# Differential attention beside a projection: each head's query tiles taken from the widest to the narrowest

## The chip, the cores and the metric

One core of a Trainium2 chip runs the whole program. The metric is the time of one execution on the device in microseconds (us); the time before is the median of three runs. Engines are written as the profile writes them: PE (TensorE, matrix products), PEld (its weight loads), DVE (VectorE), ACT (ScalarE), POOL (GpSimd), SP (the queue that issues the weight transfers).

## The reference

The program is a small model of three layers on 512 tokens of width 1024 in float32. The first layer begins with a projection `proj = rms_norm(x) @ w_in` (1952 columns), whose first part feeds a causal differential attention of 8 heads. Only this attention is touched:

```
def attn_map(qb, kk):
    sc = jnp.einsum('bhqd,bhkd->bhqk', qb, kk, ...) * scale + bias      # bias = -slope * |distance|
    return jax.nn.softmax(jnp.where(mask, sc, NEG_INF), axis=-1)
a = attn_map(qb1, k1) - lam * attn_map(qb2, k2)
o = jnp.einsum('bhqk,bhkd->bhqd', a.astype(v.dtype), v, ...)
```

Queries come in four tiles of 128. Query tile i sees keys 0 to 128*(i+1), so the score tiles are 128, 256, 384 and 512 columns wide for i = 0 to 3. Each is needed twice, for the two halves (32 features each) of a head. The value product of a head needs all four query tiles. Which of the four is computed first makes no difference to the result.

After it come a latent attention (`mla`), an output projection, a cross attention, a mixture of experts, and a second model part; none of them is edited.

## The kernel before

**Stages.** All engines run one list of stages in order; each stage has its part for PE, ACT and DVE, and each engine takes its own instructions strictly in the order written. Semaphores tie the engines together. A `Linear` stage is a projection in tiles of 128 output columns. A full tile is 24 products of 128x512 on PE (8 slices of the contraction, each as high*high L279, high*low L280, low*high L281). For each tile ACT rounds the weights of the tile after next into `w_high` (L234), DVE subtracts to get `w_low` (L240), and DVE takes the finished product out of PSUM (L675 or L678). On DVE these two stand together: `w_low` first, then the taking-out.

**Places.** The differential attention (`diff`, kind "alibi") is not a stage of its own. It is cut into 35 calls `diff.gap(n)`, n = 0 to 34, here called places. Places 0 to 25 lie in the tiles 2 to 14 of the projection "in": an even place in the middle of a tile (after 12 of its 24 products), an odd place at the end of a tile. Places 26 and 27 lie in the small tile "kpe", 28 to 31 in the projection "uq" and 32 to 34 in "ukv", whose tiles are short (6 or 3 products each). In the middle of a tile, on ACT and DVE, the place comes before the tile's `w_high`, `w_low` and taking-out; at the end of a tile it comes after them.

**What a place does.** A group is one head and one query tile, 32 in all; group n has the two score tiles of its width w. Place n does, on each engine, in this order:

- PE: the two score tiles of group n (L875, four weight loads and products of K = 32, two per score tile); the transposes of group n-2 (L887, one for each 128 columns); if group n-3 was the last of its head, the value products (L903, 8 of them).
- ACT: the copy of the transposes of group n-2 (L955); after every second head the copy of the value product (L962); the two exponentials of group n (L939).
- DVE: reciprocal, scale and combination of the probabilities of group n-1 (L1013, L1018, L1020); then for group n, for each of the two score tiles, bias plus row minimum (L996, written in place into PSUM).

**The one pair of banks.** The scores of all groups go into one pair of PSUM banks (`diff.banks = pairs[1:]`), so the score tile j of group n waits on PE until the exponential j of group n-1 has read the bank (L873, `need(pe, "att_act", ("exp", before, ...))`). PE is in order, so everything behind it waits too. Every eighth place also has four transposes of values (L713, copied at L722), and single operations of other work are hung on fixed places: angles for the later rotary embedding (L1206 to L1224, on DVE at places 4, 6, 8, 10, 12, 14), squares for norms (L388, on ACT at places 4, 12, 20), the roots of two norms with table loads on ACT (L441, L1229, place 22).

The order of the groups is the list `self.groups` in `Attention.__init__` (L742 to L746). Everything else (which place, which bank, which buffer) goes by the group's number. The last entry of a group, the list `closes`, says after which group the head's value products may run.

Of the kernel before, what the change touches and what calls it, by code (L numbers as in the profile page):

```python
# [28 lines left out]
QT = S // P  # L29
# [85 lines left out]
class Events:  # L115
# [12 lines left out]
    def done(self, ins, name, label=None, by=1):  # L128
        ins.then_inc(self.sem(name), by)
        self.count[name] = self.count.get(name, 0) + by  # L130
        if label is not None:
            self.seen[name, label] = self.count[name]
# [7 lines left out]
    def need(self, eng, name, label):  # L140
        self.wait(eng, name, self.plan[name, label])
# [7 lines left out]
def program(nc, a, plan):  # L149

    with ExitStack() as ctx:
# [94 lines left out]
        class Linear:  # L246
# [3 lines left out]
            def __init__(self, name, high, low, ready, take_act=None, take_dve=None, before=None, beside=None,  # L250
                         opening=None, middle=None):
                self.opening, self.middle = opening, middle or {}
                self.name, self.high, self.low, self.ready = name, high, low, ready
                self.beside = beside or {}
                self.take_act, self.take_dve, self.before = take_act, take_dve, before
                _, self.nt, self.kt, self.m, self.n = STAGE_OF[name]
                self.base = BASE[name]
# [471 lines left out]
        class Attention:  # L729
# [5 lines left out]
            def __init__(self, name, heads, kind, scale, scores, probs, turned, pv, out, wait_scores, wait_v,  # L735
                         next_tile, wait_out=None, per_tile=2, outs=None, after=None, lazy=False):
                self.outs, self.after, self.beside, self.wait_values = outs or (ps_o, ps_m), after, {}, {}
                self.name, self.heads, self.kind, self.scale = name, heads, kind, scale
                self.scores, self.probs, self.turned, self.per_tile = scores, probs, turned, per_tile
                self.pv, self.out, self.wait_scores, self.wait_v = pv, out, wait_scores, wait_v  # L740
                self.wait_out, self.next_tile = wait_out, next_tile
                wide_ = [(h, i) for h in range(heads) for i in range(QT)]  # L742
                if kind == "alibi":
                    self.groups = [([(h, i, 0), (h, i, 1)], (i + 1) * P,
                                    [(h, i, [(0, b) for b in range(i + 1)])], [h] if i == QT - 1 else [])
                                   for h, i in wide_]  # L746
                elif kind == "causal":
                    self.groups = [([(h, i, 0), (h + 1, i, 0)], (i + 1) * P,
                                    [(h + r, i, [(r, b) for b in range(i + 1)]) for r in range(2)],
                                    [h, h + 1] if i == 0 else [])  # L750
                                   for h in range(0, heads, 2) for i in reversed(range(QT))]
                else:
                    self.groups = [([(h, i, 0) for i in range(QT)], 2 * P,
                                    [(h, b, [(i, b) for i in range(QT)]) for b in range(2)], [h])
                                   for h in range(heads)]
                self.m0, self.h0, self.o0 = seen_groups["n"], seen_heads["n"], seen_outs["n"]
                self.u0, self.opened = [0] * len(self.groups), []
                if not lazy:
                    for n in range(len(self.groups)):
                        self.number(n)  # L760
                sizes.extend(len(group[0]) for group in self.groups)
                seen_groups["n"] += len(self.groups)
                seen_heads["n"] += heads
                seen_outs["n"] += heads // per_tile
                self.last = ("att_act", ("out", seen_outs["n"] - 1))
                self.banks = pairs
# [178 lines left out]
            def act_turn(self, act, n):  # L945
                for q, (h, i, blocks) in enumerate(self.groups[n][2]):
                    u = self.u0[n] + q
                    need(act, "turn_pe", u)
                    if n == 0 and q == 0 and self.wait_out:
                        self.wait_out(act)  # L950
                    if i == (QT - 1 if self.kind == "causal" else 0) and h >= len(self.turned):

                        need(act, "att_pe", ("values", self.h0 + h - len(self.turned)))
                    dst, src = self.place_turned(h, i, len(blocks))
                    done(act.copy(dst, src(ps_t[u % 2])), "turn_act", u)  # L955
# [2394 lines left out]
```

How the kernel before makes its waits and increments, by code:

```python
    def wait(self, eng, name, value):  # L134
        if self.waited.get((id(eng), name), 0) < value:
            eng.wait_ge(self.sem(name), value)
            self.waited[id(eng), name] = value
# [78 lines left out]
        def wait_evac(eng, t):  # L217
            eng.wait_ge(evacuated[t % BANKS], t // BANKS + 1)
# [7 lines left out]
        def wait_products(eng, name):  # L226
            eng.wait_ge(tile_done, BASE[name] + STAGE_OF[name][1])
# [1 line left out]
        def split_high(act, t):  # L229
            _, _, kt, m, _ = TILE[t]
            act.wait_ge(w_loaded[t % RING], 16 * (t // RING + 1))
            if t >= SPLIT:
                act.wait_ge(tile_done, t - SPLIT + 1)
            act.activation(WH[:, t % SPLIT, 0:kt * m], WRAW[:, t % RING, 0:kt * m],
                           ACT.Copy).then_inc(high_ready, 1)
# [1 line left out]
        def split_low(dve, t):  # L237
            _, _, kt, m, _ = TILE[t]
            dve.wait_ge(high_ready, t + 1)
            dve.tensor_tensor(WL[:, t % SPLIT, 0:kt * m], WRAW[:, t % RING, 0:kt * m],
                              WH[:, t % SPLIT, 0:kt * m].bitcast(F32), ALU.subtract).then_inc(low_ready, 1)
# [23 lines left out]
            def tensor_tile(self, pe, j):  # L265
                while scores_read:
                    need(pe, *scores_read.pop())
                t = self.base + j
                pe.wait_ge(low_ready, t + 1)
                if t >= BANKS:
                    wait_evac(pe, t - BANKS)
                out = ps_lin[t % BANKS][0:self.m, 0:self.n]
# [1687 lines left out]
        def store_y(act, b):  # L1960
            act.wait_ge(y_taken, b + 1)
            for n in range(2):
```

## Time and profile before

| what | value |
|---|---|
| device time, median of 3 runs | 2140.44 us (2137.41 to 2144.48) |
| span of the profiled execution | 2139.1 us |
| PE busy | 1953.0 us (91%) |
| DVE busy | 1079.6 us (50%) |
| ACT busy | 792.7 us (37%) |
| mean granted TensorE clock | 0.955 |

The span is the time from the first to the last instruction of one profiled execution. No device time is listed for that one execution; its span lies 1.3 us under the median of the three runs. Places 0 to 31 fall between 34.9 us and 195 us of the span, which is 7% of it. "Busy" of PE counts a product until its modelled end, so short waits between products can hide in it. PE's clock has two levels, 1.2 and 2.4 GHz, shown as a granted clock of 0.50 and 1.00.

### The profile page before, as it was taken

To read this page: it belongs to the slowest core of one execution; us is meant where nothing else is said; L and a number is where in the kernel's file an instruction comes from. 1 tells how busy PE (TensorE), PEld (TensorE's weight loads), DVE (VectorE), ACT (ScalarE), POOL (GpSimd) and SP (SyncE) were. 2 spreads that over 40 slices of the span, in tenths; PEclk is the share of its full clock that TensorE was granted. 3 is DMA by queue.
4 is the path that set the end of the run, shared out by engine and by line. 5 is a ranking of instruction groups with operands and counts; after the bars stand their busy time and mean duration, and the time that the engine had idled before them with its cause. 6 is when DMAs were issued, how large, how long until landed. Compare 5 with 4: busy or idle time off the path is not lost.

```text
span 2139.1 us, 25847 instructions
## 1 busy us (share of the span) xinstructions
PE 1953.0 (91%) x10050; PEld 1526.5 (71%) x10050; DVE 1079.6 (50%) x2000; ACT 792.7 (37%) x1653; POOL 118.9 (6%) x85
## 2 busy tenths in 40 slices
PE   7999998859877769999989999999998999999997
PEld 5665667646544457788987888788876778888886
DVE  6767655452211137685564444644556554434344
ACT  4456644532211136633543321322423643222222
POOL 0000000000000034020420000000000000000000
PEclk9999999979999969999999999999998899999999
DMA  5102313439999951112002222232220022222321
GB/s 187 35 12 79 111 55 116 149 125 387 411 412 406 405 196 60 62 67 69 1 1 68 95 99 89 90 108 90 98 93 17 1 74 94 99 98 82 107 89 48
DMA packets 78394, 261.10 MB, mean 122 GB/s; under 512 B 9377, under 2 KB 11681, under 8 KB 77889
## 3 DMA queue, kind: packets, MB, share of 16 engines
q1 hardware_dynamic: 68112, 231.47, 30.2%
q0 software_dynamic: 5040, 19.58, 2.8%
q10 hardware_dynamic: 5120, 8.39, 1.1%
q8 instruction: 81, 1.33, 0.2%
q14 instruction: 41, 0.33, 0.0%
HBM read 242.62 MB, written 16.79 MB: 121 GB/s over the span
## 4 chain that ended last, share of the span: by engine, by line
PE 71%; DMA 8%; DVE 7%; ACT 3%; issue 2%; POOL 0%; SPq 0%; ACTq 0%; DVEq 0%; POOLq 0%
PE ps_pair L279 17%; PE ps_pair L281 17%; PE ps_pair L280 17%; DMA split_acts_as_f<-w_experts 7%; PE ps_pair L875 3%; PE ps_pair L1983 3%; PE ps_turn L2491 2%; PE ps_out L903 2%; PE ps_turn L887 2%; PE ps_pair L2491 1%; PE ps_shared L903 1%; DMA w_raw<-w_mem 1%; PE ps_pair L2496 1%; PE ps_shared L1994 1%; PE ps_turn L2496 1%
## 5 line engine op out<-in xcount | busy, mean ns | idle before, releaser
L279 PE MATMUL ps_pair<-split_acts,w_high 128*128 128x512 f32 (+1 forms) x1816 | 718.0, 395 | 25.3 <-DVE split_acts L608 9.9
L281 PE MATMUL ps_pair<-split_acts,w_low 128*128 128x512 f32 (+1 forms) x1816 | 705.8, 389 | 0.0
L280 PE MATMUL ps_pair<-split_acts,w_high 128*128 128x512 f32 (+1 forms) x1800 | 699.3, 389 | 0.0
L240 DVE TENSOR_TENSOR w_low<-w_raw,w_high 128x1024 fp32r<-128x1024 f32 (+5 forms) x257 | 291.9, 1136 | 295.3 <-ACT w_high L234 293.3
L279 PEld LDWEIGHTS ps_pair<-split_acts,w_high 128*128 128x128 f32 x1816 | 344.3, 190 | 104.2 <-issue 22.3
L281 PEld LDWEIGHTS ps_pair<-split_acts,w_low 128*128 128x128 f32 x1816 | 343.9, 189 | 71.9
L280 PEld LDWEIGHTS ps_pair<-split_acts,w_high 128*128 128x128 f32 x1800 | 342.0, 190 | 66.2 <-issue 0.2
L234 ACT ACTIVATE w_high<-w_raw 128x1024 fp32r<-128x1024 f32 (+5 forms) x257 | 251.2, 978 | 193.6 <-PE ps_pair L281 168.6
L1983 PE MATMUL ps_pair<-split_acts_as_f 128*64 128x256 f32 x512 | 126.5, 404 | 40.5 <-DMA split_acts_as_f<-w_experts 39.1
L1985 PE MATMUL ps_pair<-split_acts_as_f 128*64 128x256 f32 x512 | 127.0, 405 | 0.0
L354 DVE TENSOR_TENSOR x<-x,ps_pair 128x512 f32<-128x512 f32 x80 | 55.0, 687 | 139.5 <-PE ps_pair L281 139.5
L1983 PEld LDWEIGHTS ps_pair<-split_acts_as_f 128*64 128x64 f32 x512 | 71.9, 146 | 74.3 <-issue 47.8
L939 ACT ACTIVATE g<-ps_pair,columns 128x256 f32<-128x256 f32 (+3 forms) x176 | 86.8, 506 | 40.3 <-DVE columns L996 34.5
L2157 DVE TENSOR_TENSOR g<-g,ps_pair 64x256 f32<-64x256 f32 x31 | 13.2, 425 | 172.9 <-ACT g L2097 172.8
L3039 ACT ACTIVATE split_acts<-h 128x512 fp32r<-128x512 f32 x44 | 27.9, 633 | 192.4 <-DVE h L3052 192.4
L875 PE MATMUL ps_pair<-g 64*128 64x256 f32 (+5 forms) x288 | 77.5, 471 | 13.5 <-ACT g L939 7.9
L3034 ACT ACTIVATE h<-h 128x512 f32<-128x512 f32 x44 | 27.8, 632 | 134.8 <-DVE h L3045 134.8
L955 ACT COPY split_acts_as_f<-ps_turn 128x512 f32<-128x512 f32 (+3 forms) x104 | 49.7, 507 | 70.2 <-PE ps_turn L887 65.8
L875 PEld LDWEIGHTS ps_pair<-g 32*128 32x128 f32 (+2 forms) x288 | 46.0, 207 | 37.5 <-ACT g L939 14.9
L1985 PEld LDWEIGHTS ps_pair<-split_acts_as_f 128*64 128x64 f32 x512 | 71.9, 146 | 0.0
L3049 DVE TENSOR_TENSOR h<-ps_pair,h 128x512 f32<-128x512 f32 x44 | 30.4, 691 | 73.7 <-PE ps_pair L281 73.7
L887 PEld LDWEIGHTS ps_turn<-consts,g 128*128 128x128 f32 x320 | 38.0, 149 | 34.9 <-issue 14.6
(482 smaller groups left out, 2283.4 us busy)
## 6 DMA issues: line engine op xcount, KB each, us to landing
split_acts_as_f<-w_experts SPq DMA_DIRECT2D x192, 512.0 KB, 14.0
w_raw<-w_gu SPq DMA_DIRECT2D x88, 512.0 KB, 3.4
w_raw<-w_down SPq DMA_DIRECT2D x32, 448.0 KB, 3.2
w_raw<-w_gdnin SPq DMA_DIRECT2D x26, 512.0 KB, 3.5
w_raw<-w_out SPq DMA_DIRECT2D x24, 512.0 KB, 3.5
rows_y<-scratch ACTq DMA_DIRECT2D x64, 128.0 KB, 6.3
w_raw<-w_down SPq DMA_DIRECT2D x16, 512.0 KB, 3.4
w_raw<-w_in SPq DMA_DIRECT2D x15, 512.0 KB, 3.8
```

The costliest lines, as they stand in the source:

```text
L234: act.activation(WH[:, t % SPLIT, 0:kt * m], WRAW[:, t % RING, 0:kt * m], ACT.Copy).then_inc(high_ready, 1)
L240: dve.tensor_tensor(WL[:, t % SPLIT, 0:kt * m], WRAW[:, t % RING, 0:kt * m], WH[:, t % SPLIT, 0:kt * m].bitcast(F32), ALU.subtract).then_i ...
L279: pe.matmul(out, wh[:, k, :], self.high(k), start=(k == 0), stop=False)
L280: pe.matmul(out, wh[:, k, :], self.low(k), start=False, stop=False)
L281: last = pe.matmul(out, wl[:, k, :], self.high(k), start=False, stop=(k == self.kt - 1))
L875: done(pe.matmul(self.member(self.bank(m), j, w), lhs, rhs, start=True, stop=True, skip_group_check=True), "att_pe", ("scores", m, j))
L887: last = pe.transpose(ps_t[u % 2][:, at_ * P:(at_ + 1) * P], src, ident)
L903: last = pe.matmul(self.outs[o % len(self.outs)][rows, q0:q1], lhs, self.turned[h % len(self.turned)][:, slot, src:src + q1 - q0], start=f ...
L939: done(act.activation(self.member(self.prob(n), j, w), self.member(self.bank(m), j, w), ACT.Exp, bias=COL[:, c + j:c + j + 1], scale=self. ...
L1983: pe.matmul(out[rows, 0:256], xs, w[:, at_:at_ + 256], start=(k == 0), stop=(k == KT - 1), skip_group_check=True)
L1985: last = pe.matmul(out[high_rows, 0:256], xs, w[:, at_ + 256:at_ + 512], start=(k == 0), stop=(k == KT - 1), skip_group_check=True)
L2491: last = pe.matmul(pair(bank)[:, n, :], lhs(h), rhs(h), start=True, stop=True)
```

## The change

The groups of a head now run from query tile 3 (512 columns) down to query tile 0 (128 columns). The head closes with tile 0, and the guard that keeps a head from overwriting the transposed probabilities of two heads before moves to the head's first group, now tile 3. Nothing else is edited; the sum of work is the same on every engine.

```diff
@@ -742,8 +742,8 @@
                 wide_ = [(h, i) for h in range(heads) for i in range(QT)]
                 if kind == "alibi":
                     self.groups = [([(h, i, 0), (h, i, 1)], (i + 1) * P,
-                                    [(h, i, [(0, b) for b in range(i + 1)])], [h] if i == QT - 1 else [])
-                                   for h, i in wide_]
+                                    [(h, i, [(0, b) for b in range(i + 1)])], [h] if i == 0 else [])
+                                   for h in range(heads) for i in reversed(range(QT))]
                 elif kind == "causal":
@@ -948,7 +948,7 @@
                     if n == 0 and q == 0 and self.wait_out:
                         self.wait_out(act)
-                    if i == (QT - 1 if self.kind == "causal" else 0) and h >= len(self.turned):
+                    if i == (0 if self.kind == "full" else QT - 1) and h >= len(self.turned):
 
                         need(act, "att_pe", ("values", self.h0 + h - len(self.turned)))
                     dst, src = self.place_turned(h, i, len(blocks))
```

What stands on ACT from place 4 to place 6, before. L955 is the copy of the transposes, L939 the two exponentials, L388 a square for a norm, L234 the rounding of the next weights.

```order
L955 COPY split_acts_as_f_51<-ps_turn 128x3x128
L939 ACTIVATE g,columns<-ps_pair,columns 128x128 x2
L388 ACTIVATE h<-g 128x512
L234 ACTIVATE w_high<-w_raw 128x1024
L955 COPY split_acts_as_f_51<-ps_turn 128x4x128
L939 ACTIVATE g,columns<-ps_pair,columns 128x256 x2
L955 COPY split_acts_as_f_51<-ps_turn 128x128
L939 ACTIVATE g,columns<-ps_pair,columns 128x384 x2
```

The same stretch of ACT after the change:

```order
L955 COPY split_acts_as_f_51<-ps_turn 128x2x128
L939 ACTIVATE g,columns<-ps_pair,columns 128x512 x2
L388 ACTIVATE h<-g 128x512
L234 ACTIVATE w_high<-w_raw 128x1024
L955 COPY split_acts_as_f_51<-ps_turn 128x128
L939 ACTIVATE g,columns<-ps_pair,columns 128x384 x2
L955 COPY split_acts_as_f_51<-ps_turn 128x4x128
L939 ACTIVATE g,columns<-ps_pair,columns 128x256 x2
```

The exponentials ahead of `w_high` (L234) are now 512 wide instead of 128, those behind it 384 instead of 256.

What stands on DVE at the end of the same tile (place 5), before: `w_low`, the taking-out of the product, the probabilities of group 4, the biased scores of group 5.

```order
L240 TENSOR_TENSOR w_low<-w_raw,w_high 128x1024
L675 SCALAR_TENSOR_TENSOR g<-ps_pair,columns,h 128x512
L1013 RECIPROCAL columns<-columns 128x1
L1018 SCALAR_TENSOR_TENSOR columns<-columns 128x1
L1020 SCALAR_TENSOR_TENSOR g<-g,columns 128x128
L996 ISA ps_pair,columns<-split_acts_as_f_51,ps_pair 128x256
L996 ISA columns 128x1
L996 ISA ps_pair,columns<-split_acts_as_f_51,ps_pair 128x256
L996 ISA columns 128x1
```

The same stretch of DVE after the change:

```order
L240 TENSOR_TENSOR w_low<-w_raw,w_high 128x1024
L675 SCALAR_TENSOR_TENSOR g<-ps_pair,columns,h 128x512
L1013 RECIPROCAL columns<-columns 128x1
L1018 SCALAR_TENSOR_TENSOR columns<-columns 128x1
L1020 SCALAR_TENSOR_TENSOR g<-g,columns 128x512
L996 ISA ps_pair,columns<-split_acts_as_f_51,ps_pair 128x384
L996 ISA columns 128x1
L996 ISA ps_pair,columns<-split_acts_as_f_51,ps_pair 128x384
L996 ISA columns 128x1
```

The combination of the probabilities is 512 wide instead of 128, the two biased score tiles are 384 wide instead of 256. The same holds at places 1, 9, 13, 17, 21 and 25. At places 3, 7, 11 and so on it is the other way round: 256 and 128 wide instead of 384 and 512.

## Rows read from the trace of the kernel before

**Rows 1.** The page's shares of the chain that ended last, by engine.

```profile
PE 71%; DMA 8%; DVE 7%; ACT 3%; issue 2%; POOL 0%; SPq 0%; ACTq 0%; DVEq 0%; POOLq 0%
```

**Rows 2.** Groups by form, PE, 34.9 to 200 us: busy us, mean ns, idle before.

```profile
L875 PE MATMUL ps_pair<-g 32*128 32x384 f32 x32 | 9.5, 533 | 1.3 <-ACT g L939 1.3
L875 PE MATMUL ps_pair<-g 32*128 32x512 f32 x32 | 9.0, 640 | 0.0
L875 PE MATMUL ps_pair<-g 32*128 32x128 f32 x32 | 6.3, 320 | 2.8 <-ACT g L939 2.4
L875 PE MATMUL ps_pair<-g 32*128 32x256 f32 x32 | 5.9, 426 | 0.2 <-ACT g L939 0.2
```

**Rows 3.** Timeline of PE, places 18 and 19: start us, us, operation.

```profile
118.68 0.92 PE L875 MATMUL ps_pair<-g 32*128 32x384 f32 x4
119.53 0.33 PE L887 MATMUL ps_turn<-consts,g 128*128 128x128 f32 x1
119.79 2.37 PE L903 MATMUL ps_out<-split_acts_as_f,g 128*64 128x512 f32 x8
...
125.42 1.13 PE L875 MATMUL ps_pair<-g 32*128 32x512 f32 x4
126.47 0.44 PE L887 MATMUL ps_turn<-consts,g 128*128 128x128 f32 x2
...
129.28 0.39 PE L281 MATMUL ps_pair<-split_acts,w_low 128*128 128x512 f32 x1
```

**Rows 4.** Timeline of all engines, from `w_high` of place 18 to place 20.

```profile
124.26 1.09 ACT L234 ACTIVATE w_high<-w_raw 128x1024 fp32r<-128x1024 f32 x1
...
125.38 1.23 DVE L240 TENSOR_TENSOR w_low<-w_raw,w_high 128x1024 fp32r<-128x1024 f32 x1 [4.62 <-ACT w_high L234]
126.52 0.69 DVE L678 TENSOR_TENSOR g<-ps_pair,h 128x512 f32<-128x512 f32 x1
...
127.57 0.62 DVE L1020 SCALAR_TENSOR_TENSOR g<-g,columns 128x384 f32<-128x384 f32 x1
128.10 0.69 DVE L996 CUSTOM_DVE_ANT_0 ps_pair<-split_acts_as_f,ps_pair 128x512 f32<-128x512 f32 x1
...
128.71 0.73 DVE L996 CUSTOM_DVE_ANT_0 ps_pair<-split_acts_as_f,ps_pair 128x512 f32<-128x512 f32 x1
...
128.95 0.69 ACT L939 ACTIVATE g<-ps_pair,columns 128x512 f32<-128x512 f32 x1 [1.62 <-DVE columns L996]
...
130.45 0.48 PE L875 MATMUL ps_pair<-g 32*128 32x128 f32 x2 [0.19 <-ACT g L939]
```

**Rows 5.** Timeline: the other widths on DVE and ACT.

```profile
119.63 0.56 DVE L996 CUSTOM_DVE_ANT_0 ps_pair<-split_acts_as_f,ps_pair 128x384 f32<-128x384 f32 x1 [0.21 <-PE ps_pair L875]
...
123.24 0.58 ACT L939 ACTIVATE g<-ps_pair,columns 128x384 f32<-128x384 f32 x1
...
130.88 0.75 DVE L1020 SCALAR_TENSOR_TENSOR g<-g,columns 128x512 f32<-128x512 f32 x1
```

**Rows 6.** Timeline: other work hung on places 8 and 20.

```profile
73.38 0.42 DVE L1222 TENSOR_SCALAR scratch<-g 128x512 f32<-128x512 f32 x1
...
76.21 1.22 DVE L240 TENSOR_TENSOR w_low<-w_raw,w_high 128x1024 fp32r<-128x1024 f32 x1
...
132.69 0.62 ACT L388 ACTIVATE h<-g 128x512 f32<-128x512 f32 x1
```

**Rows 7.** Timeline of ACT: the first exponential of place 0.

```profile
38.06 0.37 ACT L939 ACTIVATE g<-ps_pair,columns 128x128 f32<-128x128 f32 x1 [8.09 <-DVE columns L996]
```

**Rows 8.** Timeline of PE: place 24.

```profile
152.03 1.06 PE L875 MATMUL ps_pair<-g 32*128 32x128 f32 x4 [1.18 <-ACT g L939]
```

**Rows 9.** Timeline of PE: the first scores of the latent attention.

```profile
215.65 1.22 PE L875 MATMUL ps_pair<-g,split_acts_as_f 96*128 96x512 f32 x1 [1.29 <-ACT split_acts_as_f L1449]
```

**Rows 10.** Windows: length, busy us of PE, PEld, DVE, ACT, POOL (instructions), granted clock, DMA share, GB/s.

```profile
19.70:26.50 6.80, 6.80 (x25) 5.93 (x25) 2.90 (x8) 1.21 (x3) 0.00 (x0) 0.50 0.83 301
150.60:152.10 1.50, 0.32 (x3) 0.10 (x1) 0.03 (x1) 1.49 (x4) 0.00 (x0) 1.00 0.00 0
```

## The prediction

> **What bounds the kernel now.** I read the page's chain of work first. PE holds 71% of it and every other engine 8% or less [rows 1], so a change in the attention's order is worth what it changes in PE's waits. PE does the same products after the change. I therefore looked only at places 0 to 31 and asked where PE waits there.
>
> The groups by form answer it [rows 2]. PE waits before the scores for the exponential (L939) that frees the banks. The idle time in front of L875 is 1.3 us at the 384-wide groups, 2.8 at the 128-wide, 0.2 at the 256-wide and 0.0 at the 512-wide, 4.3 us together. More hides in the busy column. The two score tiles of a group run side by side when both may start: the 384-wide group takes 119.53 - 118.68 = 0.85 us in all [rows 3]. If the second is let go late, it alone takes the full time again. Eight undisturbed 384-wide groups would be 8 x 0.92 = 7.4 us, and the row has 9.5 us. Eight undisturbed 128-wide groups would be about 3.9 us (0.49 each, shorter than the 512-wide 1.13 of [rows 3] by 3 x 0.21) and the row has 6.3. With 0.3 for the 256-wide groups that is 4.8 us more, so PE loses about 9.1 us to this wait. Followed place by place with the walk below I get 9.9 us. It falls into three parts:
> - the 128-wide groups that open a head (places 4, 12, 20, 24, 28): 5.5 us,
> - the 384-wide groups in third position (places 2, 6, 10, 14, 22): 3.8 us,
> - the start (place 1): 0.6 us.
>
> **The change, part by part.** The sum of work of each engine stays. What moves is which width stands before an odd place (behind `w_low` and the taking-out) and which before an even one. I walk the loop that PE waits for, with steps from start to start.
>
> *Lengths.* Scores of 512 take 1.05 and of 384 0.85 [rows 3]. By the same slope (0.21 for each 128 columns) it is 0.63 for 256 and 0.42 for 128. DVE starts on scores 0.10 after they end: 119.63 - 118.68 = 0.95 [rows 3, 5]. One transpose takes 0.26, two take 0.19 [rows 3]; three or four I take as 0.31 and 0.42. From the start of two transposes to the last projection product is 129.28 - 126.47 = 2.81, and 0.32 more to the next scores [rows 3], so twelve products take 2.94. `w_low` starts 1.12 after `w_high` and takes 1.14, the taking-out 0.60, reciprocal and scale 0.45. The 384-wide combination takes 0.53, the first 512-wide biased tile 0.61, and 0.24 after it ends ACT starts the exponential, 0.68 for each 512-wide one [rows 4]. The 512-wide combination takes 0.67, the 384-wide tiles about 0.50 each and the 384-wide exponentials 0.57 [rows 5]. PE starts 0.15 after an exponential ends: 128.95 + 2 x 0.68 + 0.15 = 130.46, and the second scores start at 130.45 [rows 4].
>
> *The wait that goes.* In the old order place 3 (mod 4) has 384-wide probabilities and 512-wide scores and exponentials behind the taking-out. In [rows 4] this loop ends at 130.45, and PE was ready at 129.60 [rows 3]: a wait of 0.85. After the change these widths are 256 and 128 there, so the loop is shorter by 0.13 for the probabilities, 0.39 for the first tile (the second lies beside the first exponential) and 0.66 for the two exponentials. `w_high` in front of it stands behind 256-wide exponentials instead of 384-wide ones and comes another 0.22 earlier. That is 1.40, while PE's own path is shorter by 0.64 - 0.12 = 0.52. The room grows by 0.88, the wait was 0.85. So places 4, 12, 20 and 28 lose their wait. Place 24 keeps some: the table load in front of its exponential stays, and 1.8 us (1.18 idle, and 1.06 busy where 0.49 would do [rows 8]) becomes about 1.0. With 0.36 of small rests in places 4, 12 and 20, the first part goes from 5.5 to 1.3 us, a gain of 4.2.
>
> *The wait that comes.* Now take a head in the new order, with its 512-wide scores starting at T in the middle of a tile. The biased tiles run from T+1.15 to T+2.41, the exponentials from T+2.0 to T+3.36. Only then comes `w_high`, so `w_low` starts at T+4.48 and ends at T+5.62, the taking-out ends at T+6.22. PE has reached the end of the tile at T + 1.05 + 0.19 + 2.94 = T+4.18, two microseconds before. Behind the taking-out now stand 0.45 + 0.67 for 512-wide probabilities, to T+7.33; the first 384-wide tile, and its exponential starts at T+8.05; the second ends at T+9.20, and PE may start its second scores at T+9.35. PE is there at T + 4.18 + 0.85 + 0.26 + 2.92 = T+8.21. It waits 1.14 us. In the old order the same walk with 128, 256 and 384 gives the second scores free at T+6.9 and PE there at T+7.6, so no wait, which is what place 18 shows: 0.92 for the group, no idle time [rows 3].
>
> Other work adds to it. L388 on ACT (0.53, places 4, 12, 20) delays `w_high` and lifts places 6, 14 and 22 to about 1.5, 1.65 and 1.65. The angle steps at place 8 hold DVE for 76.21 - 73.38 = 2.83 us [rows 6], to T+5.24 instead of T+4.48, and lift place 10 to 1.9. Place 18 has the bare 1.15, place 26, with narrow weight tiles, 0.95. At the start DVE is late anyway: the first exponential starts at 38.06 [rows 7] and would now start at 38.45, being 512 wide; place 1 waits 1.1 and place 2 about 2.1. So third positions go from 3.8 to 10.9 us, a loss of 7.1, and place 1 loses 0.5.
>
> *The end.* In "uq" the tiles are short and the places far apart, so the same loop has over 0.5 us of room at each; I add nothing. In "ukv" ACT is the engine that PE waits for, up to 1.29 us before the first scores of the next attention [rows 9]. There the last group is now 128 wide, which takes 2 x 0.33 us of exponentials and 0.3 of copies off ACT, but DVE arrives there later by up to 0.9. I take -0.4, bounds 0 and -1.0.
>
> *Sum.* -4.2 + 7.1 + 0.5 - 0.4 = **+3.0 us**. Against the profiled span that is 2142.1. The median of the runs shown lies 1.3 us higher, so 2143.4, which I round to 2143.5. That is +0.14%. What a measurement of this kernel can tell from no change is about 0.3%, or 6.4 us.
>
> **The rivals.**
>
> *PE's clock falls in the new waits, and the kernel is measurably slower.* After the 3.9 us that PE waits for norm squares near 16 us, the granted clock is at its lower level, 1.2 GHz, from 19.7 to 26.5 us [rows 10]. One such stretch costs half of 6.8, 3.4 us. Against it: at place 24 PE idled 1.18 us and stayed at 1.00 [rows 8, 10]. For it: places 2, 10 and 22 now lose 1.6 to 2.1 us each. One fall makes +6.4, 2146.9, just at the bound; two make 2150. It decides from the first fall on, since +3.0 alone stays inside. The Trainium skill, "TensorE: Matmul & The Clock Gate", section "What's actually happening", has the clock gate go by how busy PE has been recently; by it the sum is 3.4 us more for each fall, by the row of place 24 nothing. Chance 0.2.
>
> *The opening waits go and nothing takes their place, a gain.* It holds if `w_low` is not late at the odd places. With it 1 us earlier the wait of 1.14 is gone, and the kernel gains 4.2 + 0.4: 2135.8. For it speaks that in the old order place 18 passes without a wait [rows 3]. Against it: ACT can't start `w_high` before a 512-wide exponential has ended, which is fixed by the order. Even so it is less than the bound; only with the spread of the runs would it show. Chance 0.12.
>
> *The waits only change places.* PE's delay at one place gives DVE and ACT time to catch up before the next, and the total stays near 9.9: 2140.4, give or take 1.5. For it: the sums of widths over a tile pair are the same in both orders. Chance 0.13.
>
> **How the numbers follow.** My forecast, wait moved and 3.0 us longer, has 0.55. Its own range is 2141 to 2146: the error of the walk is at most 0.8 over all places where I can set it beside the old trace, and the end is open by 0.6. The range for 8 in 10 goes from the middle of the gain (2138) to between one and two clock falls (2149). Slower by over 0.3%: nearly all of the clock rival plus a few hundredths of the forecast's upper tail, 0.22. Faster by over 0.3%: only the gain rival's lower tail with the spread of 7 us that three runs show, 0.06. Within 0.3%: 0.72.
>
> **What would show it right or wrong.** In the profile after, L875 at 128 columns should show almost no idle time and about 4 us busy except place 24. L875 at 256 columns should carry the idle time, ahead of it exponentials of 384 columns, with busy time well over 5.9 us, and some 13 us lost in all. L240 should start after PE has ended its tile at places 5, 9, 13, 17 and 21. The first scores of the latent attention should start near 218.6 us instead of 215.65 [rows 9]. I am wrong if the 256-wide groups start without a wait, if the clock row has a stretch at 0.50 between 40 and 200 us, or if the attention ends where it did and the time moves elsewhere.

## The result, and the profile after

The changed kernel is slower, by a little more than one measurement can tell from nothing.

| what | before | after |
|---|---|---|
| device time, median | 2140.18 us (2137.09 to 2145.57, 10 runs) | 2150.22 us (2145.91 to 2151.28, 10 runs) |
| ratio of runs taken side by side | 1 | 1.0039, 95% interval 1.003 to 1.0049 |
| span of the profiled execution | 2139.1 us | 2146.2 us |
| mean granted TensorE clock | 0.955 | 0.951 |

The ratio is +8.3 us (0.0039 x 2140), with an interval from +6.4 to +10.5. The forecast was +3.0. A slowdown of more than 0.3% was given a chance of 0.22 in all.

The groups by form of PE over the same stretch as [rows 2]: busy us, mean ns of one, idle before.

```profile
L875 PE MATMUL ps_pair<-g 32*128 32x512 f32 x32 | 9.6, 639 | 0.9 <-ACT g L939 0.9
L875 PE MATMUL ps_pair<-g 32*128 32x256 f32 x32 | 9.1, 426 | 7.1 <-ACT g L939 7.1
L875 PE MATMUL ps_pair<-g 32*128 32x384 f32 x32 | 8.0, 533 | 0.3 <-ACT g L939 0.3
L875 PE MATMUL ps_pair<-g 32*128 32x128 f32 x32 | 3.9, 321 | 0.0
```

The wait has moved as the prediction said. It left the 128-wide groups (2.8 idle and 6.3 busy before, 0.0 and 3.9 now) and the 384-wide ones, and stands at the 256-wide groups, which had 0.2 and 5.9 and now have 7.1 and 9.1.

One of these waits in full, on the timeline of all engines from the scores of place 5 to the transposes of place 6:

```profile
59.38 1.05 ACT L234 ACTIVATE w_high<-w_raw 128x1024 fp32r<-128x1024 f32 x1
59.68 0.91 PE L875 MATMUL ps_pair<-g 32*128 32x384 f32 x4
...
60.53 1.22 DVE L240 TENSOR_TENSOR w_low<-w_raw,w_high 128x1024 fp32r<-128x1024 f32 x1 [1.26 <-ACT w_high L234]
61.67 0.74 DVE L675 SCALAR_TENSOR_TENSOR g<-ps_pair,columns,h 128x512 f32<-128x512 f32 x1
...
62.77 0.75 DVE L1020 SCALAR_TENSOR_TENSOR g<-g,columns 128x512 f32<-128x512 f32 x1
63.44 0.55 DVE L996 CUSTOM_DVE_ANT_0 ps_pair<-split_acts_as_f,ps_pair 128x384 f32<-128x384 f32 x1
...
64.15 0.58 ACT L939 ACTIVATE g<-ps_pair,columns 128x384 f32<-128x384 f32 x1 [2.99 <-DVE columns L996]
64.72 0.57 ACT L939 ACTIVATE g<-ps_pair,columns 128x384 f32<-128x384 f32 x1
64.87 1.26 PE L875 MATMUL ps_pair<-g 32*128 32x256 f32 x4 [1.26 <-ACT g L939]
66.06 0.44 PE L887 MATMUL ps_turn<-consts,g 128*128 128x128 f32 x2
```

Read it upwards. The 256-wide scores wait for the 384-wide exponentials; these wait for DVE's bias tile (L996); and that stands behind the 512-wide probabilities, the taking-out and `w_low`, which starts 0.85 us after the scores of place 5 because `w_high` came late.

PE's loss at a place is taken from the trace in one way for every kernel below: the start of the first operation behind the group's scores (a transpose from place 2 on), less the start of the last product ahead of them, less 0.32 (that product), less the time that the scores take when nothing holds them (0.42, 0.63, 0.85 or 1.06 by width, rounded here). At place 6 the last product starts at 63.23, so it is 66.06 - 63.23 - 0.32 - 0.63 = 1.88. Over places 0 to 31 the changed kernel loses 13.6 us and the old one 9.9, so the waits cost +3.7.

The clock gives nearly all of the rest of what is lost ahead of the latent attention. In windows with the columns of [rows 10]:

```profile
43.80:47.20 3.40, 2.14 (x13) 1.31 (x12) 2.54 (x11) 1.26 (x5) 0.00 (x0) 1.00 0.34 133
47.20:50.60 3.40, 3.40 (x12) 2.72 (x11) 0.94 (x5) 2.92 (x7) 0.00 (x0) 0.50 0.00 0
34.90:210.00 175.10, 165.65 (x731) 104.69 (x730) 120.81 (x333) 84.03 (x224) 0.00 (x0) 0.99 0.11 32
```

The wait of place 2 lies in the first window, where PE is busy for 2.14 of 3.40 us. Behind it the granted clock is 0.50 for 3.4 us, the lower of the two levels (1.2 GHz). Such a stretch did not exist between 30 and 200 us before:

```profile
34.90:210.00 175.10, 169.55 (x759) 107.81 (x758) 122.56 (x338) 89.06 (x234) 0.00 (x0) 1.00 0.14 42
```

Half of 3.4 is 1.7 us. The first scores of the latent attention, which closed [rows 9] at 215.65, now start here:

```profile
221.31 1.22 PE L875 MATMUL ps_pair<-g,split_acts_as_f 96*128 96x512 f32 x1 [1.29 <-ACT split_acts_as_f L1449]
```

That is 5.66 later: 3.7 of waits, 1.7 of clock and 0.2 from ahead of the attention, whose first scores start at 35.07 us instead of 34.90:

```profile
35.07 1.13 PE L875 MATMUL ps_pair<-g 32*128 32x512 f32 x4
```

From the first scores of place 0 to those of the latent attention it is 186.24 us instead of 180.75, so 5.49 longer. This distance is the better measure, since the start of place 0 moves from profile to profile. The spans differ by 7.1.

### The profile page after: what moved, and what is told of

Same layout as the page of the kernel before. It is cut to its first block, busy times and chain, and to the rows that moved or that the text cites. A ratio compares the mean times of both kernels' runs of the same rounds, so it can differ in the third digit from the quotient of the medians.

```text
span 2146.2 us, 25837 instructions
## 1 busy us (share of the span) xinstructions
PE 1960.8 (91%) x10050; PEld 1530.9 (71%) x10050; DVE 1081.1 (50%) x2000; ACT 792.7 (37%) x1653; POOL 117.0 (5%) x85
## 4 chain that ended last, share of the span: by engine, by line
PE 76%; DVE 9%; DMA 8%; ACT 4%; issue 2%; POOL 0%; ACTq 0%; DVEq 0%; SPq 0%; POOLq 0%
PE ps_pair L279 18%; PE ps_pair L281 18%; PE ps_pair L280 18%; DMA split_acts_as_f<-w_experts 6%; PE ps_pair L875 4%; PE ps_pair L1983 3%; PE ps_out L903 3%; PE ps_turn L2491 2%; PE ps_turn L887 2%; PE ps_pair L2491 1%; PE ps_shared L903 1%; ACT g L939 1%; DVE ps_pair L996 1%; ACT w_high L234 1%; DVE w_low L240 1%
## 5 line engine op out<-in xcount | busy, mean ns | idle before, releaser
L234 ACT ACTIVATE w_high<-w_raw 128x1024 fp32r<-128x1024 f32 (+5 forms) x257 | 251.3, 978 | 192.1 <-PE ps_pair L281 168.6
L1983 PE MATMUL ps_pair<-split_acts_as_f 128*64 128x256 f32 x512 | 132.3, 418 | 40.7 <-DMA split_acts_as_f<-w_experts 38.1
L1985 PE MATMUL ps_pair<-split_acts_as_f 128*64 128x256 f32 x512 | 132.8, 418 | 0.0
L1983 PEld LDWEIGHTS ps_pair<-split_acts_as_f 128*64 128x64 f32 x512 | 74.5, 151 | 77.8 <-issue 46.5
L939 ACT ACTIVATE g<-ps_pair,columns 128x256 f32<-128x256 f32 (+3 forms) x176 | 86.8, 506 | 47.9 <-DVE columns L996 41.8
L875 PE MATMUL ps_pair<-g 64*128 64x256 f32 (+5 forms) x288 | 77.5, 471 | 17.4 <-ACT g L939 12.2
L955 ACT COPY split_acts_as_f<-ps_turn 128x512 f32<-128x512 f32 (+3 forms) x104 | 49.7, 507 | 69.7 <-PE ps_turn L887 65.1
L875 PEld LDWEIGHTS ps_pair<-g 32*128 32x128 f32 (+2 forms) x288 | 45.6, 207 | 41.7 <-ACT g L939 19.6
L1985 PEld LDWEIGHTS ps_pair<-split_acts_as_f 128*64 128x64 f32 x512 | 74.4, 151 | 0.0
L2097 ACT ACTIVATE g<-ps_pair 64x256 f32<-64x256 f32 x31 | 11.7, 376 | 141.0 <-PE ps_pair L1985 141.0
```

Of the source, the lines that this page charges most:

```text
L234: act.activation(WH[:, t % SPLIT, 0:kt * m], WRAW[:, t % RING, 0:kt * m], ACT.Copy).then_inc(high_ready, 1)
L875: done(pe.matmul(self.member(self.bank(m), j, w), lhs, rhs, start=True, stop=True, skip_group_check=True), "att_pe", ("scores", m, j))
L939: done(act.activation(self.member(self.prob(n), j, w), self.member(self.bank(m), j, w), ACT.Exp, bias=COL[:, c + j:c + j + 1], scale=self. ...
L1983: pe.matmul(out[rows, 0:256], xs, w[:, at_:at_ + 256], start=(k == 0), stop=(k == KT - 1), skip_group_check=True)
L1985: last = pe.matmul(out[high_rows, 0:256], xs, w[:, at_ + 256:at_ + 512], start=(k == 0), stop=(k == KT - 1), skip_group_check=True)
```

## The experiments

All ratios are to the old kernel run beside the experiment, and "later" and "earlier" speak of the first scores of the latent attention against the 215.65 of [rows 9]. Place 0 starts anywhere from 33.84 to 36.10 us in the ten profiles, so "the attention takes" gives the distance from the first scores of place 0 to the first scores of the latent attention: 180.75 us in the old kernel, 186.24 in the changed one.

### Head 0 in the old order

Only the seven other heads are turned, to see how much of the loss is the start, where DVE is late anyway. Against the changed kernel, without the line of the guard, which follows `ORDER` too:

```diff
+        ORDER = lambda h: (0, 1, 2, 3) if h == 0 else (3, 2, 1, 0)
...
-                                    [(h, i, [(0, b) for b in range(i + 1)])], [h] if i == 0 else [])
-                                   for h in range(heads) for i in reversed(range(QT))]
+                                    [(h, i, [(0, b) for b in range(i + 1)])], [h] if i == ORDER(h)[-1] else [])
+                                   for h in range(heads) for i in ORDER(h)]
```

> The changed kernel, but head 0 keeps the old order (128 to 512 columns); heads 1 to 7 run from 512 to 128. The waits at places 1 and 2 should be the old ones (0.6 and 1.4 us instead of 1.1 and 1.9), the stretch of lower granted clock at 47 us of the span should be gone, the waits at places 6, 10, 14, 18 and 22 should stay at 1.3 to 2.0 us each. Theory (waits moved to the third place of a head, plus one clock fall in head 0): 1.0 us of waits and 1.7 us of clock are given back, about 2147.5 by the median of the changed kernel. Rival (the loss comes from the order in all heads alike, the clock fall costs nothing): 2149.5. Rival (the loss is made later in the expert stage, whatever the attention does): no different from 2150.

Measured: 2147.2 us (2143.76 to 2151.37, 12 runs), ratio 1.0031 (1.002 to 1.0041), +6.6 us. The waits come to 13.1 us and the latent attention starts at 219.48. Places 1 and 2 went back to the old kernel's 0.6 and 1.4, but place 4, where an old-order head meets a 512-wide group, waits 0.8, so the waits fall by only 0.6. The clock does not fall near 47 us now; it falls once later, at 143.5 us. So most of the loss is not the start's, and where the clock falls is not tied to place 2. The median is close to the 2147.5 of the theory, but not for its reason: 0.6 us of waits came back where it had 1.0, and the fall moved where it was to go. The interval overlaps that of the changed kernel. Place 0 starts early here:

```profile
33.84 0.49 PE L876 MATMUL ps_pair<-g 32*128 32x128 f32 x4
```

The attention takes 219.48 - 33.84 = 185.64 us, 4.9 more than in the old kernel, and that is its 3.2 of added waits and 1.7 for one fall.

### `w_low` behind the attention's work, in both orders

On DVE the tiles 2 and up of the projection "in" now do the taking-out, then the place's own DVE work, and only then `w_low`. It takes `w_low` out of the loop that PE waits for. The same edit is made to the changed kernel and to the old one, in `Linear.vector`:

```diff
+                    if self.name == "in" and j > 1:
+                        self.take_dve(dve, j, self.base + j, ps_lin[(self.base + j) % BANKS][0:self.m, 0:self.n])
+                        for stage in self.beside.get(j, ()):
+                            stage.vector(dve)
+                        split_low(dve, self.base + j + AHEAD)
+                        continue
```

> The changed kernel, but in the tiles 2 to 14 of the projection in, DVE makes w_low of the tile after next only behind the place at the end of the tile, not in front of it. If w_low, late because of the 512-wide exponentials ahead of w_high, is what PE waits for in the third place of a head, the waits of 1.3 to 2.0 us there fall to 0 to 0.8 us, the 13.6 us of waits over places 0 to 31 to about 3 us, and the time by about 10 us from the changed kernel, to 2140. If only the 512-wide probabilities and 384-wide score tiles behind it count (1.11 us more DVE and ACT work in the loop than in the old order), the waits fall by less than half: 2146. If the loss sits elsewhere, no change: 2150.

> The old order, with the same move of w_low behind the place at the end of a tile. The waits should fall from 9.9 to about 2 us (place 1 at 0.7, place 24 at 1.2) and the time by about 8 us, to 2132. With e2 beside it: if w_low in the loop is what makes the two orders differ, the distance between the orders shrinks to about 1 us of waits, plus what the clock makes of them; if the order costs for another reason, it stays at 5 us or more in the first 300 us of the span.

Measured, changed order: 2134.32 us (2132.12 to 2141.02, 12 runs), ratio 0.9973 (0.9961 to 0.9984), clearly under the 2140 expected. Old order: 2134.15 us (2129.61 to 2138.44, 7 runs), ratio 0.9962 (0.9948 to 0.9976). The waits fall to 3.8 and 2.8 us, and neither has a stretch at 0.50 between 30 and 200 us. PE by form, changed order with `w_low` last (the edit moves L875 to L881, L939 to L945 and L996 to L1002):

```profile
L881 PE MATMUL ps_pair<-g 32*128 32x512 f32 x32 | 9.6, 639 | 0.2 <-ACT g L945 0.2
L881 PE MATMUL ps_pair<-g 32*128 32x384 f32 x32 | 8.0, 533 | 0.3 <-ACT g L945 0.3
L881 PE MATMUL ps_pair<-g 32*128 32x256 f32 x32 | 6.9, 427 | 0.4 <-ACT g L945 0.3
```

The 256-wide groups' 7.1 us of idle time is 0.4, and their busy time is 6.9 instead of 9.1. The timeline of place 5 shows how:

```profile
57.74 0.55 DVE L1002 CUSTOM_DVE_ANT_0 ps_pair<-split_acts_as_f,ps_pair 128x384 f32<-128x384 f32 x1
...
58.45 0.58 ACT L945 ACTIVATE g<-ps_pair,columns 128x384 f32<-128x384 f32 x1 [1.19 <-DVE columns L1002]
...
58.73 1.22 DVE L240 TENSOR_TENSOR w_low<-w_raw,w_high 128x1024 fp32r<-128x1024 f32 x1
...
59.64 0.79 PE L881 MATMUL ps_pair<-g 32*128 32x256 f32 x4
```

The bias tiles now stand ahead of `w_low`, the first exponential starts before it, and the next scores start with no wait. The places 0 and the first scores of the latent attention:

```profile
34.66 1.13 PE L881 MATMUL ps_pair<-g 32*128 32x512 f32 x4
209.73 2.93 PE L881 MATMUL ps_pair<-g,split_acts_as_f 96*128 96x512 f32 x3 [1.10 <-ACT split_acts_as_f L1455]
```

```profile
36.10 0.49 PE L881 MATMUL ps_pair<-g 32*128 32x128 f32 x4
209.67 2.93 PE L881 MATMUL ps_pair<-g,split_acts_as_f 96*128 96x512 f32 x3 [1.29 <-ACT split_acts_as_f L1455]
```

The first pair is the changed order, the second the old one. That both reach the latent attention at nearly the same moment (0.06 us apart) is chance: the old order began its places 1.44 us later in this profile. The attention takes 175.07 us in the changed order and 173.57 in the old one. So the place of `w_low` makes most of the difference between the orders: with it in the loop they are 5.5 us apart (one clock fall of 1.7 included), with it out of the loop 1.5, of which 1.0 are the waits that are left (3.8 against 2.8). Both kernels beat the one before, by some 6 and 8 us. The two kernels in the changed order are 14 us apart by their ratios (1.0039 and 0.9973); 9.8 of that are waits, and the rest fits two to three clock falls, which was not shown apart.

### The old kernel with a plain delay

The clock and the places behind the attention can change if it merely ends later. So 24 products are added to the old kernel in the output projection behind it, and nothing else.

```diff
+                    for _ in range(24 if self.name == "out" and j == 3 and k == 0 else 0):
+                        pe.matmul(out, wh[:, k, :], self.high(k), start=True, stop=True)
```

> The kernel before, with 24 more products of 128x512 on PE in tile 3 of the output projection (they write the same first partial product again, so that the result is the same), 24 x 0.228 = 5.5 us of work that keeps PE busy and moves everything behind it. If what stands behind the attention passes a shift on unchanged, the span and the median grow by 5.5 us, to 2145.7. If the stages behind (the experts, whose clock and transfers differ between executions) react to when they start, it grows by clearly more or less than 5.5, up to 10 us.

Measured: 2145.92 us (2144.11 to 2151.9, 12 runs), ratio 1.0027 (1.0017 to 1.0036), +5.8 us for 24 products, 0.23 us from start to start, which is 5.5 us. The waits of the attention stay at 9.9 us and its end at 215.65. So a delay here passes to the end about one to one, within the interval of +3.6 to +7.7 us, and what the change costs in the attention must be most of its cost.

### The waits filled with products

If the clock falls because PE waits, filling the six longest waits with products that nobody uses should bring back the clock and leave the waits' own cost. The added products read weights and activations that are there anyway and write into the bank that the place's transposes overwrite.

```diff
+                fill = {2: 6, 6: 5, 10: 6, 14: 5, 18: 3, 22: 5}.get(n, 0) if self.kind == "alibi" else 0
+                if fill:
+                    u = self.u0[n - 2]
+                    if u >= 2:
+                        need(pe, "turn_act", u - 2)
+                    tile = BASE["in"] + 2 + n // 2
+                    for _ in range(fill):
+                        pe.matmul(ps_t[u % 2][:, :], WH[:, tile % SPLIT, 0:P], hi(0), start=True, stop=True)
```

> The changed kernel, but PE fills most of the wait in front of the scores at places 2, 6, 10, 14, 18 and 22 with 3 to 6 extra products of 128x512 (0.228 us each, 30 in all) into a bank of transposes that is written anew right behind; they change no result. The waits as seen from place to place stay, only PE is busy in them. The profile of the changed kernel has one stretch of lower clock at 47 us, behind the wait at place 2. Theory (waits of 1.8 us and more let the clock fall now and then, so the attention costs more than its waits): no fall between 30 and 200 us, the attention ends 1.7 us earlier than in the changed kernel's profile (219.6 instead of 221.3), and the median is 2 to 5 us under that of the changed kernel: 2145 to 2148. Rival (the clock costs nothing beyond the one profile): 2150. Rival (the fill delays the scores): later than 2150.

Measured: 2144.27 us (2141.67 to 2148.39, 12 runs), ratio 1.0019 (1.0009 to 1.0029), +4.1 us. Place 6 on the timeline of PE, the filler at L878 and the scores at L883:

```profile
62.53 1.29 PE L878 MATMUL ps_turn<-split_acts,w_high 128*128 128x512 f32 x5
63.83 1.25 PE L883 MATMUL ps_pair<-g 32*128 32x256 f32 x4
65.02 0.66 PE L895 MATMUL ps_turn<-consts,g 128*128 128x128 f32 x4
```

Over the whole stretch, with the columns of [rows 10], and at its end:

```profile
34.90:210.00 175.10, 172.49 (x770) 110.40 (x768) 121.60 (x337) 85.02 (x227) 0.00 (x0) 1.00 0.12 36
```

```profile
220.45 2.07 PE L883 MATMUL ps_pair<-g,split_acts_as_f 96*128 96x512 f32 x2 [1.10 <-ACT split_acts_as_f L1457]
```

No stretch between 30 and 200 us is below 1.00. With 30 products more to do the kernel is 4.2 us shorter than without them (1.0019 against 1.0039), and the two intervals do not meet; that of the second measurement of the changed kernel, below, overlaps the filled one's by 0.0004. It starts the latent attention 4.8 us later than the old kernel, but its place 0 started late as well:

```profile
35.64 1.13 PE L883 MATMUL ps_pair<-g 32*128 32x512 f32 x4
```

The attention takes 184.81 us, 4.1 more than in the old kernel, of which 3.7 are the waits. Against the first profile of the changed kernel it takes 1.4 us less, with the same waits (13.6 us) and one fall less.

The Trainium skill, "TensorE: Matmul & The Clock Gate", section "What's actually happening", says that the gate follows how busy PE has lately been. The traces agree in part: 2.14 of 3.40 us busy is followed by 0.50, and with the waits filled there is no fall; but a like busy share does not always bring one: the old kernel's place 24, shown further down, has 2.10 of 3.40 and stayed at 1.00.

### `w_high` ahead of the middle place

The other half of the loop is that `w_high` stands behind the 512-wide exponentials. Here ACT does it first, in tiles 2 to 11, in `Linear.scalar`:

```diff
                 for j in range(self.nt):
+                    early = self.name == "in" and 1 < j < 12
+                    if early:
+                        split_high(act, self.base + j + AHEAD)
                     for stage in self.middle.get(j, ()):
                         stage.scalar(act)
-                    self.scalar_tile(act, j)
+                    if not early:
+                        self.scalar_tile(act, j)
```

> The changed kernel, but in the tiles 2 to 11 of the projection in, ACT makes w_high at the start of a tile, in front of the exponentials of the place in its middle. w_low stays where it is, in the loop at the end of the tile, but is no longer late. If its lateness is the cause, the waits at places 2, 6, 18 and 22 fall from 1.9, 1.9, 1.3 and 1.8 us to 0.5 or less; those at 10 and 14 stay at 1.7 to 2.0, since there the angle steps hold DVE anyway. Sum of the waits 8 instead of 13.6, time 2144 to 2145. If the 512-wide probabilities and the presence of w_low in the loop do it, whether late or not: waits stay above 11 us, 2149.

Measured: 2144.15 us (2140.02 to 2151.76, 12 runs), ratio 1.0017 (1.0005 to 1.0028), +3.6 us. PE's 256-wide groups:

```profile
L879 PE MATMUL ps_pair<-g 32*128 32x256 f32 x32 | 8.1, 429 | 3.9 <-ACT g L943 3.9
```

Places 2 and 18 lose nothing now and place 6 loses 0.7, but places 10 and 14 keep 2.1 and 1.9, and place 22 keeps its 1.8. The last is no surprise once seen: `w_low` ahead of place 22 belongs to tile 12, which the edit leaves alone, and I had expected it to go. At place 10 the angle steps ahead of `w_low` [rows 6] hold DVE whatever ACT does. The result is useful in another way. The waits come to 9.3 us, less than the old kernel's 9.9, and the latent attention still starts 2.84 us later, at 218.49. The clock falls twice, at 81.3 and 142.8 us, for 3.4 us each: -0.6 + 2 x 1.7 = 2.8. So the total of the waits does not decide. With three of them at 1.8 to 2.1 us, 9.3 us of waits cost more here than 9.9 us with one that long.

### Both kernels again

The same two kernels once more, since one profile can't say how often the clock falls.

> The changed kernel once more, for a second profile and more times. Waits of places 0 to 31 again 13.6 us, the same to 0.3 us, since they follow from the order. The stretches of lower clock between 30 and 200 us may lie elsewhere and be none to three; each moves the end of the attention by 1.7 us. If the one fall of the first profile is typical, the attention ends near 221.3 again; if the fall was an accident, near 219.6; if falls are more frequent than that profile shows, 223 or later. What the expert stage (560 to 900 us) adds may differ by 3 us either way.

> The kernel before once more, for a second profile: waits of 9.9 us in places 0 to 31, no or one stretch of lower clock in them (place 2 or 24), the first scores of the latent attention at 215.7 us. If the first profile had a lucky expert stage, the stretches of lower clock between 560 and 900 us add up to more than its 55 us, and the span is up to 3 us over 2139.

Measured, changed kernel: 2149.06 us (2142.78 to 2155.14, 12 runs), ratio 1.0038 (1.0025 to 1.005), span 2151.9. Old kernel: one run at 2137.99, span 2136.2. Windows of the changed kernel, with the columns of [rows 10]:

```profile
46.20:49.60 3.40, 3.40 (x13) 2.99 (x13) 1.27 (x5) 2.12 (x7) 0.00 (x0) 0.51 0.00 0
66.60:70.00 3.40, 3.40 (x6) 1.16 (x6) 3.29 (x8) 2.40 (x6) 0.00 (x0) 0.50 0.00 0
148.60:152.00 3.40, 3.40 (x7) 1.11 (x6) 0.73 (x4) 2.79 (x6) 0.00 (x0) 0.51 0.00 0
```

```profile
224.46 1.22 PE L875 MATMUL ps_pair<-g,split_acts_as_f 96*128 96x512 f32 x1 [1.29 <-ACT split_acts_as_f L1449]
```

The waits are the same (13.6 us), but the clock falls three times instead of once: 3.7 + 3 x 1.7 = 8.8, and 224.46 - 215.65 = 8.81. The old kernel again waits 9.9 us and has no fall in this stretch. Its latent attention starts at 216.35, 0.7 later, because its place 0 started 0.76 later. Behind the attention its two profiles also differ, by 3.0 us at 357 us, where the first has been at the low clock for 6.8 us more since 260 us, and by up to 4.9 us in the expert stage. From the first scores of the latent attention to the end, the profiles take between 1919.8 and 1927.5 us. A comparison of single spans can be off by several us, then, and the ratios have to carry the verdict.

With these runs the falls can be counted against the waits. The two profiles of the changed kernel, the one with head 0 in the old order and the one with `w_high` first have 16 waits of 1.8 us or more between them, at places 2, 6, 10, 14 and 22. All seven falls that these four profiles have between 30 and 200 us stand at the end of one of the 16 or just behind it: twice behind place 2, once each behind 6 and 10, three times behind 22, never behind 14. No fall stands behind a shorter wait of these four profiles. The old kernel has one wait of that size, 1.8 us at place 24, and stayed at the full clock behind it in all three of its profiles (the plain delay's among them). The first of them, in a window at that place:

```profile
150.00:153.40 3.40, 2.10 (x11) 1.34 (x10) 1.27 (x7) 2.54 (x5) 0.00 (x0) 1.00 0.00 0
```

PE is no busier there than ahead of the fall at 47.2 us. A wait of this size is a chance of a fall, then, not a fall.

All ten profiles together, in us. "Takes" is the distance from place 0 to the latent attention, "explained" the waits over 9.9 plus 1.7 for each fall:

| kernel | place 0 | latent attention | takes | against 180.75 | waits | falls | explained |
|---|---|---|---|---|---|---|---|
| old | 34.90 | 215.65 | 180.75 | 0 | 9.9 | 0 | 0 |
| old, again | 35.66 | 216.35 | 180.69 | -0.1 | 9.9 | 0 | 0 |
| old, plain delay behind | 34.97 | 215.65 | 180.68 | -0.1 | 9.9 | 0 | 0 |
| old, `w_low` last | 36.10 | 209.67 | 173.57 | -7.2 | 2.8 | 0 | -7.1 |
| changed | 35.07 | 221.31 | 186.24 | +5.5 | 13.6 | 1 | +5.4 |
| changed, again | 34.89 | 224.46 | 189.57 | +8.8 | 13.6 | 3 | +8.8 |
| changed, head 0 old | 33.84 | 219.48 | 185.64 | +4.9 | 13.1 | 1 | +4.9 |
| changed, `w_low` last | 34.66 | 209.73 | 175.07 | -5.7 | 3.8 | 0 | -6.1 |
| changed, filled | 35.64 | 220.45 | 184.81 | +4.1 | 13.6 | 0 | +3.7 |
| changed, `w_high` first | 34.97 | 218.49 | 183.52 | +2.8 | 9.3 | 2 | +2.8 |

The two that are off by 0.4 (`w_low` last in the changed order, and filled) have a fall of 6.8 us that begins further ahead of the latent attention than in the others, and 0.25 us more between the last transposes and its first scores.

## Why the prediction was right on the waits and wrong on the clock

**The loop and its lengths: right.** The walk gave 13.3 us of waits in the changed kernel and the trace has 13.6. By parts: places 2, 6, 10, 14, 18, 22 and 26 were put at 10.9 and lose 11.0; place 1 was put at 1.1 and loses 1.06; the openings were put at 1.3 and lose 1.6 (place 24 1.2, place 28 0.4). The closeness of the total is in part luck, since single places missed in both directions: place 26 was put at 0.95 and loses 0.16, while place 6 was put at 1.5 and loses 1.89, places 14 and 22 at 1.65 and lose 1.89 and 1.80, and place 28 was to lose nothing. The old kernel's 9.9 was right as well. The experiment with `w_low` last confirms the mechanism: once it has left the loop, 9.8 of the 13.6 us go, and 7.1 of the old order's 9.9.

**The end: wrong by 0.4.** I took -0.4 for "ukv". Waits, clock and the later start of place 0 explain the whole 5.66 us, with no gain at the end. This is inside the bounds given (0 to -1.0).

**The clock: the step that failed.** The sum had no term for the clock, and a stretch at 0.50 between 40 and 200 us was named as a sign that I am wrong; it came. The prediction set against a fall that "at place 24 PE idled 1.18 us and stayed at 1.00", and gave the rival 0.2. That one place stayed up was read as a rule, where it was one draw: place 24 loses 1.8 us in all, much like the new waits of 1.8 to 2.0, and behind 16 waits of that size in the reordered kernels the clock fell seven times. The old order has one of them, the new one five (places 2, 6, 10, 14 and 22), so at 7 in 16 each an execution has 2.2 falls, and one without any is rare (9/16 to the fifth, 0.06). This is an estimate: it takes the five waits as alike and independent, while place 22 had three falls behind four such waits and place 14 none behind four. The chance of the rival should have been well over a half. The price was wrong the other way: the one stretch that was read was 6.8 us long and was priced at 3.4, these are 3.4 long and cost 1.7. The filled kernel, which has none, says the same from the times: it is 4.2 us shorter, which is two to three falls, and the intervals leave room for one to four.

The old trace also held a sign for the rival that I passed over. Ahead of the latent attention PE waits three times within 5 us, the third time as shown in [rows 9], and the clock falls there:

```profile
211.24 0.66 PE L713 MATMUL ps_turn<-consts,split_acts_as_f 128*128 128x128 f32 x4 [0.84 <-ACT split_acts_as_f L349]
213.70 0.66 PE L713 MATMUL ps_turn<-consts,split_acts_as_f 128*128 128x128 f32 x4 [1.81 <-ACT split_acts_as_f L349]
```

```profile
210.90:214.30 3.40, 1.25 (x8) 0.84 (x8) 2.16 (x2) 3.33 (x7) 1.40 (x2) 1.00 0.60 165
214.30:221.10 6.80, 5.51 (x8) 2.52 (x8) 1.99 (x6) 2.81 (x7) 0.00 (x0) 0.50 1.00 358
```

No single wait there is longer than 1.81 us. It would not have settled the chance, since PE is less busy there than at the new waits (1.25 us of 3.40), but it stands against place 24.

**The total.** +3.7 of waits and 2.2 x 1.7 of clock give 7.4; measured 8.3 (6.4 to 10.5). My forecast of +3.0 with its own range of 2141 to 2146 is below that. The range for 8 in 10, up to 2149, holds the ratio (2140.4 + 8.3 = 2148.7) only by the room that it left for clock falls, and not the median of 2150.22. The clock rival, which stood on the right side of the bound, is what happened, with two smaller falls where it counted one or two large ones.

**The other rivals.** A gain needed `w_low` not to be late; it was (60.53 against PE's 59.68), and with `w_low` out of the way the gain appeared (0.9973). That the waits only change places is refuted by 13.6 against 9.9, the same in two profiles.

**Open.** How often the clock falls in an execution that isn't profiled was not counted, only inferred from the ratios and from a rate of 7 in 16 that rests on four profiles. What makes one wait lower the clock and the next not was not tried either. What moves the start of place 0 by up to 2.3 us between profiles, and the rest of the program behind the latent attention by up to 7.7, lies outside the stretch read here. What is left between the orders once `w_low` is out of the loop was not taken apart either.

## What to carry to other kernels

When one engine is the bound and waits on a loop through others, look for work in that loop that the loop does not need: here `w_low`, needed a tile later, cost 7.1 us of waits in one order and 9.8 in the other, more than the 3.7 between the orders, and moving it brought them from 5.5 to 1.5 us apart. Price a new wait twice, once for its own length and once for what the clock may do behind it, and look at the longest waits and not at their total alone, since a smaller total with three long pieces was slower; that the clock stayed up behind one wait in one profile is little evidence that it will behind five. Before two profiles are compared at one moment, take off the difference in their start: without that, two kernels that are 1.5 us apart looked equal. A walk from start to start with lengths from the old trace was good to 0.3 us in all over thirty places, and to 0.8 at the worst single one.

## What the runs showed of the hardware

The clock's fall is not fixed to a place: with waits that agree to 0.1 us it came at 47.2 us in one profile and at 46.2, 66.6 and 148.6 us in another. Behind the waits of 1.8 to 2.1 us at the places it lasted 3.4 us each time, while the wait of 3.9 us at the start is followed by 6.8 [rows 10]. The length does not go by the longest wait alone: ahead of the latent attention, where no wait is over 1.81 us but three follow each other, it is 6.8 too. And products without use made the kernel shorter: 30 of them, some 7 us of PE at the full clock, in waits that were there anyway, brought the ratio from 1.0039 to 1.0019.
